# mLSTM by chunks of 128 tokens with a carried state, in a hybrid decoder layer on one core

## The chip, the core and the metric

The kernel runs on one NeuronCore of a Trainium2 chip (trn2). Time is device microseconds (us) of one execution. The engines are TensorE (matmuls into the eight PSUM banks), VectorE, ScalarE and GpSimd (element work) and SyncE (SP), which here only issues DMAs. Each runs its own instruction queue in order; they meet at semaphores. The input is one sequence of 512 tokens of width 1024, all of it float32.

## What is computed

One decoder layer. The normalised input is projected once (`z = rms_norm(x) @ w_in`, 2964 columns) and split between three mixers: MoBA attention (4 heads of 64), an mLSTM (4 heads, q and k of 64, v of 128) and NSA attention (4 query heads of 64; compressed, selected and window branches). Their outputs are normalised by head, projected by `w_out`, and a squared-ReLU MLP of width 4096 follows. The change concerns the mLSTM. By head, with `logf` the log sigmoid of the forget gate and `ig` the input gate:

```
bcum = cumsum(logf)
D[t,s] = bcum[t] - bcum[s] + ig[s]              for s <= t
m[t]  = max(running maximum carried in, max_s D[t,s])
S[t,s] = (q_t . k_s / 8) * exp(D[t,s] - m[t])
hid_t = sum_s S[t,s] v_s / max(|sum_s S[t,s]|, exp(-m[t]))
y_ml  = head_norm(hid) * g * sigmoid(lo)
```

The reference states the same thing in chunks of 64: within a chunk the products above, and for everything earlier a state `C = sum_s exp(...) v_s k_s^T` (128 x 64, and its row for the denominator) that is decayed and added to from chunk to chunk, and multiplied with q_t and a weight of t.

## The kernel before

Tokens lie in NT = 4 tiles of 128. Every engine has one function (`@block.tensor`, `@block.vector`, `@block.scalar`, `@block.gpsimd`, `@block.sync`) in which all its work stands in the order in which it runs; nothing plans it, and the position of a call in these functions is its place in the engine's queue. A wait (`wait_ge`) holds all that is behind it on that engine.

Large float32 products are made of three products of rounded halves (fp32r), `mm3` (lines 1748 to 1752): each weight chunk is loaded into `raw` by SP, ScalarE writes its high half (`high_half`, line 763) and GpSimd the difference (`low_half`, line 661). The mixers' q and k get halves in the same way: `nq_high`/`nq_low` and `moba_high`/`moba_low`, and SP copies halves from one half of the partitions to the other (lines 559 to 604). SP's order is: chunk c of `CHUNK_ORDER`, where chunk c waits for the low half of chunk c - 2 (line 516), the four copies to `nq_st` ahead of `C_WO + 2`, then the MoBA copies in the order of `MB_ORDER` (k, k, q, q, k, k, q, q), then the MLP's weights. TensorE's first MoBA score waits for the first four of these and their low halves (`score`, line 1913).

The input projections are "jobs", each in PSUM bank job % 8; `bank_free(n)` makes TensorE wait until the reader of job n - 8 (`READER`) has read. Around the change TensorE does: MQ (two jobs of 24 matmuls), `spread` 0 and 1 (the running maximum m of a head, put on all partitions), MK, `spread` 2 and 3, the 64 products of the compression MLP, and then mLSTM in eight units u = (pair of heads p, token tile i):

- `ml_scores(u)` (line 1888): for each j <= i and both heads the 128 x 128 tile k_j . q_i;
- VectorE multiplies with the decay tiles `exp(gcol[s] - m[t])` into `probsT` (line 1409). ScalarE made these for all j <= i (line 873), GpSimd masks the diagonal ones (line 696);
- `ml_values(u)` (line 1899): for each j <= i and both heads `probsT_j` times v_j with a column of ones (129 columns), summed in PSUM;
- ScalarE copies to `hid` (`ml_evict`) and sums squares (`ml_squares`).

Between these units stand the rest of the compression (`fold`, GELU, the two small products with `w2k` and `w2v` in unit 3), the compressed attention scores (after unit 4), and the first four scores of attention. On ScalarE the high halves of w_out chunks 0 and 1 (`C_WO`, `C_WO + 1`) stand in units 3 and 4, and on GpSimd their low halves come right after `nq_low`.

Then comes the attention loop over 24 units (six pairs of heads, four token tiles each): scores, row maximum on VectorE, exponential on ScalarE, transposes, copies of them (one on VectorE, one on ScalarE, `copy_t`), and per pair values, a transposition back and the output. Pairs 0 to 3 are NSA's, pairs 4 and 5 MoBA's. In its first units the loop also carries the compressed branch (`cmp_transposes`, `cmp_out`, `cmp_gated`) and the mLSTM's divisors (`ml_divisors`, unit 2) and reciprocal roots (units 3 and 4). Their last product is the scale factors by which GpSimd multiplies `hid` and `y` (lines 726 to 732), and in ScalarE's queue `moba_high` of the q halves waits for these. After the loop come w_out's projection and the MLP.

## Time and profile before

| | us |
|---|---|
| median of 3 runs (612.62 to 613.42) | 612.93 |
| the profiled execution | 612.87 |
| its span, first to last instruction | 611.1 |
| TensorE busy, 3158 matmuls | 598.2 (98%) |
| VectorE busy | 384.7 (63%) |
| ScalarE busy | 303.1 (50%) |
| GpSimd busy | 258.3 (42%) |

Busy time of TensorE counts the pipelined end of each matmul, so it is not TensorE at its peak. An fp32 matmul has two records in the trace, an fp32r or bf16 matmul and a transpose one. In a timeline, neighbouring instructions of one kind are merged (x16), and the length of a merged line reaches to the end of its last instruction, which overlaps the start of the next line.

### The profile page before, as it was taken

The numbers are of one execution on the slowest core, as the hardware profiler recorded it, in microseconds if no ns is written. First come the engines' busy times: TensorE is split into PE (matmuls) and PEld (weight loads), VectorE is DVE, ScalarE is ACT, GpSimd is POOL, SyncE is SP. The second block draws the span as 40 slices with busy tenths as digits, with TensorE's granted clock in tenths as the row PEclk, the third lists the DMA queues.
The fourth block names the chain that finished last, engine by engine and source line by source line (L and its number), as shares of the span: only waits on it lengthen the run. The fifth ranks groups of instructions, "written<-read, shape, count | busy, mean of one in ns | idle before, by whom it ended". The sixth has DMA issues, their size and how long they took to land.

```text
span 611.1 us, 8442 instructions
## 1 busy us (share of the span) xinstructions
PE 598.2 (98%) x3158; PEld 491.5 (80%) x3158; DVE 384.7 (63%) x650; ACT 303.1 (50%) x551; POOL 258.3 (42%) x149
## 2 busy tenths in 40 slices
PE   8999999999999999999999999999999999999995
PEld 5898888877866678889888888888888888888884
DVE  6414505216787883883899868577495685771657
ACT  7613424237868952564564625545445255453322
POOL 8553413614837430053159372533722725711611
PEclk9999999999999999999999999999999999999998
DMA  9743272345412230025225070440612503204002
GB/s 331 279 151 121 96 180 86 69 104 173 146 28 65 74 105 1 0 70 201 77 86 190 24 252 0 146 130 1 213 62 110 166 2 137 70 1 168 4 35 104
DMA packets 36004, 65.08 MB, mean 106 GB/s; under 512 B 2812, under 2 KB 23548, under 8 KB 34940
## 3 DMA queue, kind: packets, MB, share of 16 engines
q1 hardware_dynamic: 35660, 64.15, 32.7%
q8 instruction: 25, 0.41, 0.3%
q10 hardware_dynamic: 304, 0.39, 0.2%
q14 instruction: 15, 0.12, 0.1%
HBM read 60.08 MB, written 2.10 MB: 102 GB/s over the span
## 4 chain that ended last, share of the span: by engine, by line
PE 91%; DVE 4%; issue 2%; ACT 1%; DMA 1%; SPq 0%; POOLq 0%; POOL 0%; DVEq 0%; ACTq 0%
PE ps L1750 20%; PE ps L1752 20%; PE ps L1751 20%; PE ps L2156 7%; PE ps L2158 7%; PE ps L2157 7%; PE ps L2028 2%; PE ps L2013 1%; PE ps L1908 1%; ACT probs L942 1%; DMA x_land<-in_x_turned 1%; PE ps L1932 1%; PE ps L1933 1%; DVE probsT L1409 1%; PE ps L1884 1%
## 5 line engine op out<-in xcount | busy, mean ns | idle before, releaser
L1750 PE MATMUL ps<-xT_h,ring_h 128*128 128x512 f32 (+1 forms) x384 | 143.6, 374 | 0.0
L1752 PE MATMUL ps<-xT_h,ring_l 128*128 128x512 f32 (+1 forms) x384 | 143.2, 373 | 0.0
L1751 PE MATMUL ps<-xT_l,ring_h 128*128 128x512 f32 (+1 forms) x384 | 143.1, 373 | 0.0
L747 POOL TENSOR_TENSOR ring_l<-raw_d,ring_h 128x1024 fp32r<-128x1024 f32 x25 | 67.3, 2699 | 129.8 <-ACT ring_h L1021 129.8
L747 POOL TENSOR_TENSOR ring_l<-raw,ring_h 128x1024 fp32r<-128x1024 f32 x31 | 76.7, 2501 | 77.6 <-DVE xres L1566 38.1
L667 POOL TENSOR_TENSOR ring_l<-raw,ring_h 128x512 fp32r<-128x512 f32 (+2 forms) x26 | 64.1, 2486 | 77.3 <-ACT ring_h L772 77.3
L1660 DVE TENSOR_TENSOR y<-ps,y 128x512 f32<-128x512 f32 x90 | 61.1, 688 | 51.0 <-PE ps L2158 50.7
L1750 PEld LDWEIGHTS ps<-xT_h,ring_h 128*128 128x128 f32 x384 | 72.4, 188 | 13.1 <-issue 0.4
L1752 PEld LDWEIGHTS ps<-xT_h,ring_l 128*128 128x128 f32 x384 | 72.4, 188 | 12.9
L1751 PEld LDWEIGHTS ps<-xT_l,ring_h 128*128 128x128 f32 x384 | 72.4, 189 | 12.8
L2156 PE MATMUL ps<-ring_h,a_h 128*128 128x512 f32 x196 | 76.7, 391 | 0.1
L2158 PE MATMUL ps<-ring_h,a_l 128*128 128x512 f32 x196 | 76.4, 390 | 0.0
L2157 PE MATMUL ps<-ring_l,a_h 128*128 128x512 f32 x196 | 76.4, 390 | 0.0
L1750 PE MATMUL ps<-ring_h,xT_h 128*128 128x512 f32 (+1 forms) x158 | 61.0, 386 | 0.3 <-DVE xT_l L1222 0.3
L1752 PE MATMUL ps<-ring_h,xT_l 128*128 128x512 f32 (+1 forms) x158 | 60.3, 381 | 0.0
L1751 PE MATMUL ps<-ring_l,xT_h 128*128 128x512 f32 (+1 forms) x158 | 60.2, 381 | 0.0
L1021 ACT ACTIVATE ring_h<-raw 128x1024 fp32r<-128x1024 f32 x32 | 33.1, 1057 | 22.8 <-PE ps L2158 19.1
L2156 PEld LDWEIGHTS ps<-ring_h,a_h 128*128 128x128 f32 x196 | 36.8, 188 | 8.5 <-issue 0.8
L1058 ACT ACTIVATE ps<-ps 128x512 f32<-128x512 f32 x32 | 18.7, 583 | 50.1 <-PE ps L1752 50.1
L2158 PEld LDWEIGHTS ps<-ring_h,a_l 128*128 128x128 f32 x196 | 36.8, 188 | 8.0
L2157 PEld LDWEIGHTS ps<-ring_l,a_h 128*128 128x128 f32 x196 | 36.8, 188 | 7.7
L772 ACT ACTIVATE ring_h<-raw 128x2048 fp32r<-128x2048 f32 (+1 forms) x14 | 26.0, 1858 | 27.0 <-PE ps L1752 16.2
(264 smaller groups left out, 1012.3 us busy)
## 6 DMA issues: line engine op xcount, KB each, us to landing
raw<-in_w_mlp SPq DMA_DIRECT2D x16, 1024.0 KB, 5.5
raw_d<-in_w_mlp SPq DMA_DIRECT2D x16, 1024.0 KB, 6.0
raw<-in_w_groups SPq DMA_DIRECT2D x8, 1024.0 KB, 4.8
raw<-in_nsa_cmp_w SPq DMA_DIRECT2D x8, 512.0 KB, 6.6
raw<-in_w_groups SPq DMA_DIRECT2D x8, 256.0 KB, 5.2
xres<-in_x SPq DMA_DIRECT2D x4, 512.0 KB, 7.2
raw<-in_w_out SPq DMA_DIRECT2D x2, 1024.0 KB, 7.3
raw<-in_w_out SPq DMA_DIRECT2D x4, 512.0 KB, 4.6
```

The costliest lines, as they stand in the source:

```text
L667: last = nc.gpsimd.tensor_tensor(ring_l[r][:, a:a + step], raw[c % RAW][:, a:a + step], ring_h[r][:, a:a + step].bitcast(F32), ALU.subtract)
L747: nc.gpsimd.tensor_tensor(slot(ring_l, n), slot_source(n), slot(ring_h, n).bitcast(F32), ALU.subtract).then_inc(lo_done, 1)
L772: nc.scalar.activation(ring_h[r][:, 0:n], raw[c % RAW][:, 0:n], ACT.Copy).then_inc(hi_done, 1)
L1021: nc.scalar.activation(slot(ring_h, n), slot_source(n), ACT.Copy).then_inc(hi_done, 1)
L1058: nc.scalar.activation(tile, tile, ACT.Relu).then_inc(relu_ready, 1)
L1660: nc.vector.tensor_tensor(ya, ps[:, product_bank(b, k) + s, :], ya, ALU.add).then_inc(acc_ready, 1)
L1750: nc.tensor.matmul(o, sh, mh, start=start, stop=False)
L1751: nc.tensor.matmul(o, sh, ml, start=False, stop=False)
L1752: return nc.tensor.matmul(o, sl, mh, start=False, stop=stop)
L2156: nc.tensor.matmul(o, ah, wh[:, q, :], start=fresh and q == 0, stop=not fresh, **go_on)
L2157: nc.tensor.matmul(o, ah, wl[:, q, :], start=False, stop=not fresh, **go_on)
L2158: last = nc.tensor.matmul(o, al, wh[:, q, :], start=False, stop=not fresh or q == 1, **go_on)
```

## The change

The mLSTM's pairs of different token tiles (j < i) are replaced by a state. For each head and each of the first three chunks (NCH = 3) the change forms the chunk's sum of k times v with weights relative to m at the chunk's end (`mend`), adds it to the decayed state before it, and multiplies the state with q times `exp(mend - m[t])` (`q_far`). The diagonal tiles (j = i) stay as they are, now with one decay tile per head and tile (`W`).

- Projection part: the order on TensorE is MQ's first half, all four `spread`, MQ's second half, six transposes of k (`key_transposes`), the diagonal score tiles (`near_scores`), MK's first half, the states (`states`), MK's second half, compression. The job numbers and thereby the PSUM banks and their readers are new.
- ScalarE makes four decay tiles and three exponentials in place in PSUM for each head; VectorE the differences of m at chunk ends, `q_far`, the weighted keys `k_tok`, the product of near scores and decay in place in `W`, and the carried states.
- mLSTM part: `ml_values(u)` is one near product and (i > 0) one far product a head. Two units share one eviction; ScalarE copies to `hid` and writes squares to `hid_sq`, and VectorE sums them (`ml_sums`).
- Compression: GELU, the products with `w2k` and `w2v` and the compressed values come after all mLSTM units and after the first four attention scores. The compressed scores are in one bank (bank 6), with full-height products, inside the attention loop behind the first transposes; their maxima and probabilities on VectorE are in units 0 and 1 of the loop, `cmp_transposes` and `cmp_out` behind steps 4, 6 and 8 instead of 1, 3 and 6, `cmp_gated` in units 3 and 4 instead of 2 and 3.
- w_out's chunks: ScalarE's high half of chunk 0 is behind the second eviction, that of chunk 1 in loop unit 4. GpSimd's low halves of chunks 0 and 1 stand behind the mLSTM's normalisation. The first two `moba_high` are in loop units 1 and 3.

The diff, cut to what the prediction speaks of:

```diff
+J_LV, J_B, J_CONV, J_LO, J_LI, J_LF, J_KV, J_KS, J_NQ, J_GC, J_SP, J_KT, J_SC, J_ST, J_H = (
+    0, 4, 8, 12, 16, 17, 18, 19, 20, 22, 24, 29, 31, 36, 39)
+J_MQ, J_MK = (23, 28), (35, 38)
+HT_BANK = 7
...
-READER = "vvvv" "vvvv" "vvvv" "aaaa" "v" "v" "v" "v" "vv" "a" "vv" "aa" "vv" "aa" "vv"
+READER = "vvvv" "vvvv" "vvvv" "aaaa" "v" "v" "v" "v" "vv" "a" "v" "vvvv" "v" "vv" "vvvv" "v" "vv" "v" "vv"
...
-ML_BANK = [2, 0]
+ML_BANK = [3, 5, 3, 5]
...
-CT_S, CO_S = 1, (3, 6)
+CS_S, CT_S, CO_S = 0, 4, (6, 8)
...
-                last.then_inc(w_ready, 1)
-            pool.wait_ge(w_ready, HEADS)
-            nq_low(2)
-            nq_low(3)
-            low_half(C_WO)
-            low_half(C_WO + 1)
+                nc.gpsimd.affine_select(out=W[:, h], in_=W[:, h], compare_op=ALU.is_ge, fill=0.0, base=0,
+                                        pattern=[[0, NT], [1, P]], channel_multiplier=-1).then_inc(w_ready, 1)
+            for h in range(HEADS):
+                nq_low(h)
+
...
-            pool.wait_ge(lo_done, split_no(C_WO) + 2)
             for n in range(2):
                 moba_low(n)
 
@@ -730,6 +736,9 @@
                 pool.wait_ge(ml_h, t + 1)
                 yml = y[:, t, 256:768].rearrange("p (h d) -> p h d", h=HEADS)
                 nc.gpsimd.tensor_tensor(yml, yml, hid[:, t, :, 0:DV], ALU.mult).then_inc(ml_y, 1)
+            low_half(C_WO)
+            low_half(C_WO + 1)
+            pool.wait_ge(lo_done, split_no(C_WO) + 2)
             for n in range(2, 2 * HEADS):
...
-                act.wait_ge(job_done, J_MB[h] + 1)
-                for j in range(NT):
-                    last = nc.scalar.activation(decay(h, slice(j, NT), j),
-                                                ps[:, J_MB[h] % 8, j * P:SEQ].rearrange("p (i t) -> p i t", t=P),
-                                                ACT.Exp, scale=-1.0, bias=gcol[:, j, h:h + 1])
-                last.then_inc(read_a, 1)
-                act.wait_ge(read_a, reads(J_MB[h])[1])
-                nc.scalar.activation(zero1[:], zero1[:], ACT.Copy).then_inc(w_exp, 1)
...
+                r, held = half_rows(h % 2), ps[:, (J_SP + h) % 8, :]
+                act.wait_ge(job_done, J_SP + h + 1)
+                act.wait_ge(mend_ready, h + 1)
+                for i in range(NT):
+                    last = nc.scalar.activation(W[:, h, i, :], held[:, i * P:(i + 1) * P], ACT.Exp, scale=-1.0,
+                                                bias=gcol[:, i, h:h + 1])
+                last.then_inc(w_exp, 1)
+                act.wait_ge(w_exp, h + 1)
+                for i in range(1, NT):
+                    last = nc.scalar.activation(held[r, i * P:(i + 1) * P], held[r, i * P:(i + 1) * P], ACT.Exp, scale=-1.0,
+                                                bias=mend[r, h, i - 1:i])
+                last.then_inc(far_ready, 1)
+            nc.scalar.activation(factor[:], factor[:], ACT.Exp).then_inc(factor_ready, 1)
+            act.wait_ge(job_done, J_MK[1] + 1)
...
+            for h in range(HEADS):
+                nq_high(h)
+            act.wait_ge(dup_in, 32)
+            for k, keys_ in enumerate((kselT, kwinT)):
+                nc.scalar.activation(nk_st[:, k, :], keys_[:], ACT.Copy).then_inc(nk_hi, 1)
+
...
+            def ml_evict(v):
+                p, i = ml_place(v)
+                act.wait_ge(ml_o, v + 1)
+                nc.scalar.activation(hid[:, i:i + 2, 2 * p:2 * p + 2, :], ml_pair(v, DV + 1), ACT.Copy)
+                if v >= 2:
+                    act.wait_ge(ml_ss, v - 1)
+                nc.scalar.activation(hid_sq[:, v % 2], ml_pair(v, DV), ACT.Square).then_inc(ml_used, 1)
...
-            for u in range(len(ML_UNITS)):
-                if u >= 1:
-                    ml_evict(u - 1)
-                if u == 1:
+            for v in range(4):
+                if v == 3:
                     act.wait_ge(gelu_arg, 1)
                     nc.scalar.activation(cg[:, 3], cg[:, 2], ACT.Exp, scale=-1.5957691216057308).then_inc(gelu_exp, 1)
-                if u == 3:
-                    act.wait_ge(kv_cmp, 1)
-                    nc.scalar.activation(kcT[:], ps[:, 4, 0:NP_], ACT.Copy).then_inc(kc_ready, 1)
-                if u in (3, 4):
-                    high_half(C_WO + u - 3)
-                if u == 5:
-                    act.wait_ge(cs_sub, 1)
-                    nc.scalar.activation(cexp[:], cexp[:], ACT.Exp).then_inc(cs_exp, 1)
-                if u >= 1:
-                    ml_squares(u - 1)
-                if u >= 6:
-                    moba_high(u - 6)
+                ml_evict(v)
+                if v == 1:
+                    high_half(C_WO)
...
             exp(0)
-            ml_evict(len(ML_UNITS) - 1)
+            act.wait_ge(kv_cmp, 2)
+            for m in range(2):
+                last = nc.scalar.activation(kc2[half_rows(m), m, :], ps[half_rows(m), 6, 0:NP_], ACT.Copy)
+            last.then_inc(kc_ready, 1)
             exp(1)
...
                 if u == 0:
+                    act.wait_ge(cs_sub, 1)
+                    nc.scalar.activation(cexp[:], cexp[:], ACT.Exp).then_inc(cs_exp, 1)
+                if u in (1, 3):
+                    moba_high(u // 2)
+                if u == 4:
+                    high_half(C_WO + 1)
+                if u == 2:
...
+            for h in range(HEADS):
+                p, m = divmod(h, 2)
+                r, bank = half_rows(m), (J_SP + h) % 8
+                dve.wait_ge(job_done, J_SP + h + 1)
+                link(nc.vector.tensor_copy(mend[:, h, :], ps[:, bank, P - 1:NCH * P:P]))
+                nc.vector.tensor_tensor(into[:, :, h], gcol[:, 0:NCH, h], ps[:, bank, P - 1:NCH * P:P], ALU.subtract)
+                nc.vector.tensor_tensor(on[r, p, :], ps[r, bank, P - 1:2 * P:P], mend[r, h, 1:NCH], ALU.subtract
+                                        ).then_inc(mend_ready, 1)
+            for h in range(HEADS):
+                p, r = h // 2, half_rows(h % 2)
+                dve.wait_ge(far_ready, h + 1)
+                nc.vector.tensor_tensor(q_far[p][r, :], ps[r, (J_SP + h) % 8, P:SEQ], qkT[r, p, P:SEQ], ALU.mult).then_inc(read_v, 1)
...
+            for h in range(HEADS):
+                dve.wait_ge(job_done, J_SC + h + 1)
+                dve.wait_ge(w_ready, h + 1)
+                nc.vector.tensor_tensor(W[:, h], ps[:, (J_SC + h) % 8, :].rearrange("p (i t) -> p i t", t=P), W[:, h],
+                                        ALU.mult).then_inc(read_v, 1)
...
-            for u, (p, i) in enumerate(ML_UNITS):
-                w = (i + 1) * P
-                for m in range(2):
-                    s, h = 2 * u + m, 2 * p + m
-                    dve.wait_ge(ml_s, u + 1)
-                    dve.wait_ge(w_ready, h + 1)
-                    if s >= 3:
-                        dve.wait_ge(ml_o, (s - 3) // 2 + 1)
-                    nc.vector.tensor_tensor(probsT[:, s % 3, 0:w].rearrange("p (j t) -> p j t", t=P),
-                                            ps[:, ML_BANK[u % 2] + m, 0:w].rearrange("p (j t) -> p j t", t=P),
-                                            decay(h, i, slice(0, i + 1)), ALU.mult).then_inc(ml_p, 1)
...
+            def ml_sums(v):
+                p, i = ml_place(v)
+                c = SS_ML + HEADS * i
+                dve.wait_ge(ml_used, v + 1)
+                nc.vector.tensor_reduce(stat[:, c:c + 2 * HEADS].rearrange("p (i h) -> p i h", h=HEADS)[:, :, 2 * p:2 * p + 2],
+                                        hid_sq[:, v % 2], AX.X, ALU.add).then_inc(ml_ss, 1)
+
+            ml_sums(0)
+            gelu()
+            ml_sums(1)
+            gelu_rest()
+            ml_sums(2)
+            ml_sums(3)
             row_max(0)
             row_max(1)
-            cmp_probs()
+            cmp_values()
             row_max(2)
...
-                if u in (2, 3):
-                    cmp_gated(u - 2)
+                if u == 0:
+                    cmp_max()
+                if u == 1:
+                    cmp_probs()
+                if u in (3, 4):
+                    cmp_gated(u - 3)
...
             def spread(h):
 
-                bank_free(J_MB[h])
-                if h == 0:
-                    pe.wait_ge(m_ready, 2)
...
+                bank_free(J_SP + h)
+                nc.tensor.matmul(ps[:, (J_SP + h) % 8, :], sel[:, h, :], m_split[:, 0, :], start=True, stop=False)
+                nc.tensor.matmul(ps[:, (J_SP + h) % 8, :], sel[:, h, :], m_split[:, 1, :], start=False, stop=True).then_inc(job_done, 1)
...
+                for i in range(NT):
+                    t = slice(i * P, (i + 1) * P)
+                    for m in range(2):
+                        r = half_rows(m)
+                        last = nc.tensor.matmul(ps[:, (J_SC + 2 * p + m) % 8, t], qkT[r, 2 + p, t], qkT[r, p, t], start=True, stop=True)
+                        if i == NT - 1:
+                            last.then_inc(job_done, 1)
...
+                for c in range(NCH):
+                    for m in range(2):
+                        h = 2 * p + m
+                        last = nc.tensor.matmul(ps[half_rows(m), (J_ST + p) % 8, (DV + 1) * c:(DV + 1) * (c + 1)],
+                                                k_tok[:, c, DH * h:DH * h + DH], lv1[:, c, h, :], start=True, stop=True)
+                last.then_inc(job_done, 1)
+
+            half_feature(J_MQ[0], C_MQ, 0)
+            pe.wait_ge(m_ready, 2)
+            for h in range(HEADS):
+                spread(h)
+            half_feature(J_MQ[1], C_MQ, 1)
+            pe.wait_ge(silu_done, 4)
+            key_transposes(0)
+            key_transposes(1)
+            near_scores(0)
+            near_scores(1)
+            half_feature(J_MK[0], C_MK, 0)
+            states(0)
+            states(1)
+            half_feature(J_MK[1], C_MK, 1)
+
...
-                pe.wait_ge(ml_p, 2 * u + 2)
-                if u == 1:
-                    pe.wait_ge(*reads(J_MB[3]))
-                if u >= 2:
-                    pe.wait_ge(ml_used, u - 1)
+                t = slice(i * P, (i + 1) * P)
+                if u in (4, 6):
+                    pe.wait_ge(ml_used, u // 2 - 1)
...
                 for m in range(2):
-                    for j in range(i + 1):
-                        last = nc.tensor.matmul(ps[:, 7 - u % 2, 256 * m:256 * m + DV + 1],
-                                                probsT[:, (2 * u + m) % 3, j * P:(j + 1) * P],
-                                                lv1[:, j, 2 * p + m, :], start=(j == 0), stop=(j == i))
-                last.then_inc(ml_o, 1)
+                    h = 2 * p + m
+                    last = nc.tensor.matmul(ml_tile(u, DV + 1)[:, m, :], W[:, h, i, :], lv1[:, i, h, :], start=True, stop=i == 0, **far)
...
+                        last = nc.tensor.matmul(ml_tile(u, DV + 1)[:, m, :], q_far[p][r, (i - 1) * P:i * P], state[r, p, i - 1, :],
+                                                start=False, stop=True, skip_group_check=True)
+                if u % 2:
+                    last.then_inc(ml_o, 1)
...
-            pe.wait_ge(read_v, reads(J_H)[1])
+            pe.wait_ge(*reads(J_MK[1]))
+            for u in range(4):
+                ml_values(u)
+            pe.wait_ge(*reads(J_H))
...
-
-            for u in range(len(ML_UNITS)):
-                if u + 1 < len(ML_UNITS):
-                    ml_scores(u + 1)
-                if u == 3:
...
+            for u in range(4, len(ML_UNITS)):
                 ml_values(u)
-                if u == 4:
-                    pe.wait_ge(kc_ready, 1)
...
-                if u == 6:
-                    pe.wait_ge(nk_lo_ready, 2)
-                    pe.wait_ge(nq_in, 16 * HEADS)
-                    pe.wait_ge(ml_p, 14)
-                    score(0)
-                    score(1)
-                if u == 7:
-                    score(2)
-                    score(3)
+            pe.wait_ge(nk_lo_ready, 2)
+            pe.wait_ge(nq_in, 16 * HEADS)
+            for s in range(4):
+                if s == 1:
+                    pe.wait_ge(ml_used, 3)
+                score(s)
+            pe.wait_ge(ml_used, 4)
+            pe.wait_ge(gelu_ready, 1)
...
+            def cmp_scores():
+                pe.wait_ge(kc_ready, 1)
+                pe.wait_ge(vc_ready, 1)
+                nc.tensor.matmul(ps[:, 6, :], identb[:], mask_c[:, :, 0:1, :].to_broadcast([P, NT, HEADS, NP_]), start=True, stop=True)
+                for i in range(NT):
+                    for p in range(2):
+                        c = (HEADS * i + 2 * p) * NP_
+                        last = nc.tensor.matmul(ps[:, 6, c:c + 2 * NP_], nqT[:, p, i * P:(i + 1) * P],
+                                                kc2[:].rearrange("p m n -> p (m n)"), start=False, stop=True, skip_group_check=True)
+                last.then_inc(cs_done, 1)
 
...
+                    if s == CS_S:
+                        cmp_scores()
                     if s == CT_S:
                         cmp_transposes()
                     if s in CO_S:
```

## Rows read from the trace of the kernel before

**Rows 1.** The page's busy time of each engine.
```profile
PE 598.2 (98%) x3158; PEld 491.5 (80%) x3158; DVE 384.7 (63%) x650; ACT 303.1 (50%) x551; POOL 258.3 (42%) x149
```

**Rows 2.** The page's chain of waits that ended last, by engine.
```profile
PE 91%; DVE 4%; issue 2%; ACT 1%; DMA 1%; SPq 0%; POOLq 0%; POOL 0%; DVEq 0%; ACTq 0%
```

**Rows 3.** Busy us by stage: PE, PEld, DVE, ACT, POOL, then PEclk, DMA share, GB/s.
```profile
142.00:164.00 22.00, 20.98 (x213) 18.74 (x214) 15.92 (x41) 15.33 (x49) 14.64 (x15) 1.00 0.45 138
...
176.60:197.50 20.90, 18.52 (x139) 12.83 (x136) 17.35 (x39) 16.72 (x49) 16.88 (x14) 1.00 0.19 45
197.50:221.80 24.30, 23.68 (x181) 16.91 (x180) 19.30 (x44) 22.15 (x60) 10.00 (x8) 1.00 0.38 109
```

**Rows 4.** Groups of TensorE instructions: line, shapes, count, busy us, mean ns.
```profile
L1908 PE MATMUL ps<-lv,probsT 128*128 128x129 f32 x80 | 11.1, 285 | 1.0 <-DVE probsT L1409 0.8
...
L1895 PE MATMUL ps<-qkT 64*128 64x128 f32 x80 | 6.6, 292 | 0.0
...
L1976 PE MATMUL ps<-kcT,nqT 64*128 64x32 f32 x32 | 2.0, 274 | 0.0
```

**Rows 5.** Timeline of TensorE, 137 to 165 us: start, length, line, records.
```profile
137.28 3.68 PE L1884 MATMUL ps<-raw,blk 64*32 64x256 f32 x128
140.90 0.49 PE L1895 MATMUL ps<-qkT 64*128 64x128 f32 x4
...
151.26 2.05 PE L1908 MATMUL ps<-lv,probsT 128*128 128x129 f32 x16
...
158.50 1.16 PE L1895 MATMUL ps<-qkT 64*128 64x128 f32 x16
...
164.61 0.42 PE L1932 MATMUL ps<-nk_st,nq_st 128*128 128x384 f32 x1
```

**Rows 6.** Timeline of ScalarE, 126 and 151 us.
```profile
126.69 1.76 ACT L873 ACTIVATE W_own<-ps,gcol 128x512 f32<-128x512 f32 x4
...
150.83 1.90 ACT L772 ACTIVATE ring_h<-raw 128x2048 fp32r<-128x2048 f32 x1
```

**Rows 7.** Timeline of VectorE, 148 to 177 us.
```profile
147.95 0.22 DVE L1337 TENSOR_SCALAR cg<-cg 128x128 f32<-128x128 f32 x1
...
149.65 0.36 DVE L1343 COPY gelr<-gel 128x128 f32<-128x128 f32 x2
...
177.00 0.17 DVE L1513 TENSOR_TENSOR stat<-stat,den 128x16 f32<-128x16 f32 x1
```

**Rows 8.** Timeline of GpSimd, 152 to 190 us.
```profile
152.87 9.89 POOL L667 TENSOR_TENSOR ring_l<-raw,ring_h 128x512 fp32r<-128x512 f32 x8 [6.51 <-ACT ring_h L772]
...
177.32 1.04 POOL L729 TENSOR_TENSOR hid<-hid,stat 128x512 f32<-128x512 f32 x1 [11.31 <-DVE stat L1513]
...
185.67 1.19 POOL L732 TENSOR_TENSOR y<-y,hid 128x512 f32<-128x512 f32 x1
186.82 2.67 POOL L718 TENSOR_TENSOR mq_lo<-mqT,mq_st 64x512 fp32r<-64x512 f32 x2
```

**Rows 9.** Timeline of TensorE, the first MoBA score.
```profile
197.52 0.36 PE L1932 MATMUL ps<-mk_st,mq_st 128*128 128x256 f32 x1
```

**Rows 10.** Timeline of SP's DMA issues, 166 to 190 us.
```profile
166.54 0.60 SPq L598 DMA_DIRECT2D mk_odd<-mk_odd  x1
188.13 1.85 SPq L602 DMA_DIRECT2D mq_st<-mq_lo  x2
```

**Rows 11.** DMA issues: target, source, count, KB, median us to landing.
```profile
mk_odd<-mk_odd SPq DMA_DIRECT2D x1, 128.0 KB, 4.4
...
nq_st<-nq_lo SPq DMA_DIRECT2D x4, 128.0 KB, 5.5
...
mq_st<-mq_lo SPq DMA_DIRECT2D x4, 128.0 KB, 2.2
```

**Rows 12.** The same columns at the end; the third last is PEclk.
```profile
604.00:605.00 1.00, 0.62 (x6) 0.42 (x4) 0.97 (x3) 0.73 (x1) 0.72 (x1) 1.00 0.91 340
...
606.00:607.00 1.00, 0.00 (x0) 0.00 (x0) 0.81 (x4) 0.16 (x1) 0.00 (x0) 0.80 0.00 0
```

257 lines of the change are left out of this document (110 added, 147 removed).

## The prediction, as it was written before the result

> **What bounds the kernel now.** I read the page's busy shares first. TensorE is busy for 598.2 of 611.1 us [rows 1] and the chain that ended last lies on it for 91% [rows 2], so time is won only where TensorE gets shorter or where its few waits go. The profiled execution took 612.87 us, 1.8 us more than its span; the median of the three runs is 612.93, so the sum can be made against 612.87. Second came the busy time by stage. The mLSTM stretch (142 to 164 us) has TensorE busy for 20.98 of 22.00 us; the first pairs of attention (176.6 to 197.5) for 18.52 of 20.90; the last ones, to the output projection, for 23.68 of 24.30 [rows 3]. The reader is to see that nothing idles for long, and that the attention loop has VectorE, ScalarE and GpSimd at 65% to 90% as well: work that is put into the loop finds little room. Third I read the order of each queue by the timelines, because this kernel has every order written out by hand, and the change moves work past other work on GpSimd.
>
> **TensorE's own work.** Removed: 40 score products and 40 value products, each an fp32 matmul in two records, 80 + 80 records. A run of 16 value records takes 2.05 us, of which the last one's 0.28 overlaps: about 0.12 us a record, 9.6 us in all; 16 score records take 1.16 us because two 64-row products run side by side: 0.06 us a record, 4.8 us in all [rows 4, 5]. Added: 16 near scores (32 records, 1.9 us), 16 near values (32 at 0.12, 3.8 us), 12 far values in 64-row pairs (24 at 0.06, 1.4 us), 12 state products, 64 columns wide, side by side as the scores are (24 at 0.06, 1.4 us; 2.8 if they don't overlap), 6 transposes (0.11 each, 0.7 us). That is 14.4 against 9.2: 5.2 us less. The compressed scores go from 32 records in 2.0 us [rows 4] to 16 full-height records that I put at 0.12 each, equal. With these numbers alone the kernel would end near 607.7.
>
> **The projection part.** Transposes, near scores and states now stand before the compression: +4.3 us with a switch of operand type, so compression ends at about 145.3 instead of 141.0 [rows 5]. New waits there: the MK bank of the first half is the bank of the last spread, and is free only when VectorE has multiplied the last head's exponentials with q. ScalarE does seven exponentials of 128 columns a head; four with 1280 columns together took 1.76 us [rows 6], so at most 2.0 us a head, from 120.1 (spread done) to 128.1, VectorE until 128.7; TensorE comes to it at 128.9. Hidden, with 0.2 us to spare; without that cover up to 2 us are lost. VectorE's mends, key and decay products (some 6 us) lie beside 11 us of the two MK halves, on an engine with long waits there; nothing for that. The masks on GpSimd are one 512-column instruction instead of four small ones: nothing.
>
> **From compression to the loop.** TensorE has 2.75 (units 0 to 3) + 1.0 (fold) + 2.75 (units 4 to 7) + 1.45 (scores 0 to 3) = 8.0 us to do: it would be at 153.3. What is late is the GELU chain, which lay beside mLSTM work before. The exponential of GELU stands on ScalarE behind three double evictions (about 1.2 us each, copy and square) and behind the 1.90 us high half of the first w_out chunk [rows 6]: I get 153.3 for its end. VectorE's rest of GELU lasts from 147.95 to 150.0 in the trace, 2.05 us [rows 7]: 155.4. Then the two small products (1.2), VectorE's last two sums of squares, row maxima and four copies of compressed values (3.5 us with the wait for the first softmax exponential): 158.9, where TensorE can begin the compressed scores (2.2). From here VectorE is the chain: maxima and subtraction 1.3, unit 1 of attention 1.6, compressed probabilities 2.0, units 2, 3 and 4 with divisors, gated sums and reciprocal roots 2.4 + 3.4 + 3.2. That puts the mLSTM scale factors (stat, line 1513) at 175.0; before they are there at 177.2 [rows 7]. So of 5.2 us some 2 are left by then; the others are turned into waits of 1 to 2 us each. Bounds: 169.3 if none of these waits is there (154.5 for the loop's start, 12.6 from there to the factors as between 164.61 and 177.2 [rows 5, 7], 2.2 for the compressed scores); 177.5 if the loop keeps the length it has. The wait for nq_st: the last copy is issued at about 147.8 and takes 2.2 us (as on an empty queue) to 5.5 [rows 11], TensorE asks at 151.9; up to 1.4 us, inside these bounds.
>
> **GpSimd's order: the term that decides.** Before, the low halves of the first two w_out chunks ran on GpSimd at 152.87 to 162.8, 9.89 us beside the mLSTM [rows 8]. Now they stand behind the mLSTM normalisation and ahead of the low halves of MoBA's queries. Normalisation starts when the factors are there and takes from 177.32 to 186.86, 9.5 us; then, before, the two q halves follow at once and TensorE reads the first MoBA score at 197.52 [rows 8, 9], 5.4 us after their copies landed (two issued from 188.13 to 189.98, 2.2 us each [rows 10, 11]). After: 175.0 + 0.1 + 9.5 = 184.6; two low halves, 10.0: 194.6. This holds SP too. Its queue has w_out chunk 3 behind the low half of chunk 1, and all MoBA copies behind that. Before, chunk 3 was issued at 162.8, and the last of the four MoBA copies behind it went out at 166.54 and landed 4.4 us later, at 170.9: 8.1 us after the release [rows 10, 11]. After, six copies are behind it instead of four, but they don't wait for GpSimd in between: 8 to 9 us, I take 8.3. The last q copy lands at 194.6 + 8.3 = 202.9. TensorE would come to that score at about 196: it stands for 6 to 7 us, and the score is at 202.9 instead of 197.52, +5.4. Behind it the order is as before: 24.3 us to the projection with TensorE 97% busy, so next to nothing is caught up; w_out chunks 2 and 3 keep 4 us of slack, as ScalarE and GpSimd shift with the loop.
>
> **The clock.** In the trace the granted clock is at 2.4 GHz (1.00) through all working stretches; after the last matmul, over at 604.6, it falls to 1.2 GHz within 606 to 607: that slice has 0.80 [rows 12]. The new stop is three times as long as those 2 us, so I expect the fall inside it. What it costs afterwards no row shows; from nothing (it rises at once) to 3 us (half speed for as long as the stop lasted). I take 0.8.
> The Trainium skill (TensorE: Matmul & The Clock Gate, What's actually happening) says that the throttled state is the default and activity releases it, so work resumes slow. By that rule the cost is above nothing, and the sum moves toward the upper half of my range; the trace agrees as to the fall.
>
> Sum: 612.87 + 5.4 + 0.8 = **619.1 us**.
>
> **The rivals.**
> *The saving reaches the end.* The 5.2 us, perhaps less 1 or 2 for new waits: 607.7 to 611.5, faster. For it speaks TensorE's 98%. It needs the last q copy by 197.5 - 3, thus the factors by 167, while even without a wait they come at 169.3. It decides only if GpSimd's 9.5 + 10.0 us or the 8.3 behind them shrink by 5 us. 8%.
> *Neither way.* Factors at 169.3 to 170 and a quick landing give 612 to 613.5. 4%.
> *The stop is there but short.* Factors at 171 to 173, copies 7.5 us after the release, no fall of the clock: +1.5 to +3.5, 614 to 616.4. 18%.
> *The stop and more.* The exponentials on ScalarE take longer than 2.0 us a head, TensorE stands before MK and the whole chain shifts; or the clock costs its 3 us: 621.5 to 624. 10%.
> *As summed*, 60%, with its own range of 616.5 to 621.5.
>
> **How the numbers follow.** The likeliest is 619.1. A range of 614.5 to 622.3 holds the sum's own range, most of the short stop and a part of the long one, and leaves out the two cases below it and the top. What a measurement of this kernel tells from no change is about 0.2%, 1.2 us (611.7 to 614.1). Faster is the first rival, 8%; the same 4%; slower 88%.
>
> **What would show it.** Right: TensorE idle by 5 us or more before the first score with mk_st, ended by a transfer (mq_st); GpSimd's two low halves between the normalisation and mq_lo; SP's w_out chunk 3 issued at about 194.6; the granted clock under 1.00 just there; factors at 173 to 177; compression over at 145 to 146; a wait before the products that read gel, and one before the compressed scores. Wrong: MoBA's first score before 198, a wait over 1 us in the projections, or mLSTM records that cost more than 0.12 us.

## The result: slower, 623.03 us

The changed kernel takes 623.03 us (622.18 to 626.64, four runs) against 612.77 for the kernel before on the same chip: ratio 1.0177, 95% interval 1.0136 to 1.0218. The forecast was 619.1 with a range to 622.3, so the direction and the place of the loss were forecast, and the time lies 0.7 us above the range. The profiled execution took 622.87 us, 10.0 more than that of before.

The busy shares of the page come first, as in [rows 1]:
```profile
PE 596.7 (96%) x3099; PEld 489.2 (79%) x3099; DVE 388.9 (63%) x665; ACT 299.8 (48%) x529; POOL 257.1 (41%) x137
```
TensorE is busy for only 1.5 us less, to which the lower clock described below adds some 3.6, and its share falls from 98% to 96%. The chain of waits has new members beside it; in [rows 2] GpSimd had no share:
```profile
PE 87%; POOL 4%; DMA 3%; DVE 2%; issue 2%; ACT 1%; SPq 1%; POOLq 0%; ACTq 0%; DVEq 0%
```
Where it is lost, the timelines of GpSimd and of SP's queue show, from the mLSTM normalisation on (compare [rows 8, 10]):
```profile
175.75 1.04 POOL L735 TENSOR_TENSOR hid<-hid,stat 128x512 f32<-128x512 f32 x1 [1.69 <-DVE stat L1546]
...
184.12 1.18 POOL L738 TENSOR_TENSOR y<-y,hid 128x512 f32<-128x512 f32 x1
185.26 10.40 POOL L683 TENSOR_TENSOR ring_l<-raw,ring_h 128x512 fp32r<-128x512 f32 x8
195.73 2.61 POOL L725 TENSOR_TENSOR mq_lo<-mqT,mq_st 64x512 fp32r<-64x512 f32 x2
```
```profile
190.28 6.28 SPq L543 DMA_DIRECT2D raw<-in_w_out  x4
196.61 1.11 SPq L609 DMA_DIRECT2D mk_st<-mk_st  x2
...
199.06 1.24 SPq L618 DMA_DIRECT2D mq_st<-mq_lo  x2
```
and TensorE's at the first MoBA score (197.52 without a wait in [rows 9]):
```profile
205.50 0.55 PE L2000 MATMUL ps<-mk_st,mq_st 128*128 128x256 f32 x1 [9.30 <-DMA mq_st<-mq_lo]
```
The low halves of w_out stand between the normalisation and the MoBA queries, w_out's loads between them and the copies, and TensorE idles for 9.30 us. The score is 8.0 us late. Then comes the clock. The columns are as in [rows 3], the third last is the granted clock:
```profile
196.00:205.50 9.50, 0.20 (x3) 0.03 (x1) 1.69 (x3) 1.74 (x6) 7.30 (x6) 0.70 0.93 243
205.50:208.00 2.50, 2.50 (x13) 2.31 (x13) 1.14 (x3) 0.78 (x2) 0.00 (x0) 0.50 0.50 125
208.00:209.50 1.50, 1.50 (x10) 1.41 (x9) 0.42 (x1) 0.84 (x3) 0.00 (x0) 0.50 0.00 0
209.50:211.00 1.50, 1.50 (x13) 1.45 (x12) 0.63 (x2) 0.46 (x2) 0.00 (x0) 0.83 0.00 0
```
TensorE resumes at 1.2 GHz and stays there for about 4.5 us. A transposition of y, first in the kernel before and then here, starts 9.8 us late, so 1.8 us came after the score:
```profile
227.88 1.03 PE L2043 MATMUL ps<-ident,y 128*128 128x128 f32 x8
```
```profile
237.71 1.03 PE L2099 MATMUL ps<-ident,y 128*128 128x128 f32 x8
```
8.0 + 1.8 are the 10.0 but for 0.2.

The same columns for the projections show a second fall, which I did not foresee. The last line is the kernel before, which has 1.00 in each of the three stretches:
```profile
118.00:121.00 3.00, 3.00 (x13) 1.95 (x12) 2.20 (x13) 1.18 (x5) 3.00 (x2) 1.00 0.10 17
121.00:124.00 3.00, 3.00 (x9) 2.32 (x9) 0.93 (x3) 2.94 (x12) 1.26 (x3) 0.55 0.42 125
124.00:127.00 3.00, 3.00 (x14) 2.39 (x13) 0.85 (x2) 2.93 (x12) 0.78 (x2) 0.89 1.13 223
```
```profile
121.00:124.00 3.00, 3.00 (x15) 2.22 (x13) 0.00 (x0) 0.00 (x0) 0.08 (x1) 1.00 0.47 115
```
TensorE is busy throughout. What is new just before is that all eight matmuls of `spread`, which have four rows, stand in a row (the first at 118.43), where before they stand in two groups of four. Eight of the matmuls after them are 0.43 us apart instead of 0.23, and the compression ends at 146.9 instead of the predicted 145.3.

### The profile page after: what moved, and what is told of

The parts are those of the page before. It is cut to its first block, busy times and chain, and to the rows that moved or that the text cites. A ratio compares the mean times of both kernels' runs of the same rounds, so it can differ in the third digit from the quotient of the medians.

```text
span 621.1 us, 8286 instructions
## 1 busy us (share of the span) xinstructions
PE 596.7 (96%) x3099; PEld 489.2 (79%) x3099; DVE 388.9 (63%) x665; ACT 299.8 (48%) x529; POOL 257.1 (41%) x137
## 4 chain that ended last, share of the span: by engine, by line
PE 87%; POOL 4%; DMA 3%; DVE 2%; issue 2%; ACT 1%; SPq 1%; POOLq 0%; ACTq 0%; DVEq 0%
PE ps L1783 20%; PE ps L1785 20%; PE ps L1784 20%; PE ps L2212 7%; PE ps L2214 7%; PE ps L2213 7%; POOL ring_l L683 2%; PE ps L2069 1%; DMA nq_st<-nq_lo 1%; DMA mq_st<-mq_lo 1%; POOL nq_lo L700 1%; POOL y L738 1%; PE ps L2084 1%; POOL hid L735 1%; DMA x_land<-in_x_turned 1%
## 5 line engine op out<-in xcount | busy, mean ns | idle before, releaser
L1020 ACT ACTIVATE ring_h<-raw 128x1024 fp32r<-128x1024 f32 x32 | 33.1, 1056 | 22.8 <-PE ps L2214 19.3
```

The costliest lines, as they stand in the source:

```text
L1020: nc.scalar.activation(slot(ring_h, n), slot_source(n), ACT.Copy).then_inc(hi_done, 1)
```

## The experiments

Theory A is the prediction's: the place of the two low halves on GpSimd, and of w_out's loads on SP, makes the stop. Rival B: one of the two orders alone decides. Theory F came with the trace: matmuls of four rows and new waits let the clock fall. Theories C, D, E, G and others are named in the expectations. "Before" in each result is the kernel before on the same chip, and a ratio is against it. Each kernel has one profile, of one of its executions.

**The one move by itself, in the kernel before.** The low halves go behind the normalisation; nothing else of the change is in it.
```diff
             nq_low(3)
-            low_half(C_WO)
-            low_half(C_WO + 1)
...
-            pool.wait_ge(lo_done, split_no(C_WO) + 2)
             for n in range(2):
                 moba_low(n)
...
+            low_half(C_WO)
+            low_half(C_WO + 1)
+            pool.wait_ge(lo_done, split_no(C_WO) + 2)
             for n in range(2, 2 * HEADS):
                 moba_low(n)
```


> The kernel before, with the low halves of w_out chunks 0 and 1 moved on GpSimd behind the mLSTM normalisation, and nothing else. Theory A (this one move makes the stop, whatever form the mLSTM has): factors at 177.2, normalised at 186.8, low halves until 197.2, last q copy 9.8 us later at 207: first MoBA score at 206.5 to 207.5 instead of 197.5, then 1.2 GHz for some 4.5 us: 623 to 625.5 us. Rival D (the stop needs the new mLSTM order too): 613 to 617 us.

Measured: 624.27 us against 612.87, ratio 1.018 (1.0165 to 1.0195). TensorE's timeline in it:
```profile
206.69 0.55 PE L1932 MATMUL ps<-mk_st,mq_st 128*128 128x256 f32 x1 [9.14 <-DMA mq_st<-mq_lo]
```
Two calls in another place, with the wait that belongs to them, make the whole loss (11.4 us here, 10.3 for the change), stop and slow clock (0.50 from 204 to 212) with it; what else the change does adds nothing to it on balance.

**GpSimd's order alone.** In the changed kernel `moba_low(2)` and `moba_low(3)` go ahead of the low halves.

> The changed kernel, with the low halves of MoBA's first two q heads moved ahead of the two w_out low halves on GpSimd; SP's order is left. Theory A (two gates: GpSimd's order, and SP's queue in which the copies stand behind w_out chunk 3): the q halves are ready at 188 but the copies still wait for the low half of w_out chunk 1, which is 2.7 us later (198.4): first MoBA score at 206 to 208.5, 623 to 626 us. Rival B (GpSimd's order alone): the stop is gone, score at 196, 611 to 613 us.

Measured: 626.44, ratio 1.0206 (1.0172 to 1.0240). The query halves are done at 187.7, and the score is later still, at 208.29 after a stop of 12.28 us: SP's copies stand behind w_out chunk 3, whose release is now 2.5 us later.

**SP's order alone.** The first four heads' copies go ahead of the loads of w_out chunks 2 and 3.

> The changed kernel, with the first four heads' MoBA copies moved ahead of w_out chunks 2 and 3 in SP's queue; GpSimd's order is left. Theory A: the copies wait only for the q low halves (198.3), score at 200.5 to 202.5, a stop of 4 to 6 us instead of 9.3: 617 to 620 us. Rival B: SP's order is no gate, 622 to 623.5 us as before. Rival C (the transfers themselves are slow whatever stands before them, 4 to 6 us): score at 203 to 204, 620 to 621.5.

Measured: 621.49 (619.40 to 622.80), ratio 1.0123 (1.0091 to 1.0156), above the 617 to 620 of theory A. The stop is halved all the same:
```profile
204.53 0.55 PE L2005 MATMUL ps<-mk_st,mq_st 128*128 128x256 f32 x1 [4.55 <-DMA mq_st<-mq_lo]
```
With no load and no other copy ahead of them the two q copies land 2.2 us after their issue, so the transfers are not slow by themselves, as rival C had it. The time gains less than the stop, because the profiled execution has a slow clock at 157 to 168 besides (0.50 in 162 to 168), and reaches the score's place 3.8 us later than the changed kernel's does.

**Both orders.**

> Both moves together. Theory A: the first MoBA score comes at 196 without a stop or a fall of the clock; the second pair's k and q (low halves now at 198.4 to 203.6, copies behind w_out chunk 3) are late by 2 to 4 us for the fifth pair's first score at about 205: 612.5 to 616.5 us. Rival (the stop has another cause, such as the mLSTM factors or the loop's own pace): 619 us or more.

Measured: 618.24 (612.63 to 621.37, ten runs), ratio 1.0062 (1.0030 to 1.0095), above the 612.5 to 616.5 expected. The score comes at 198.69 with no wait. Rival B falls: there are two gates. With GpSimd's order alone the stop grows to 12.28 us, with SP's alone it is 4.55, with both it is gone. A smaller one has moved to the second MoBA pair, as expected:
```profile
210.37 0.35 PE L2007 MATMUL ps<-mk_st,mq_st 128*128 128x256 f32 x1 [2.43 <-DMA mq_st<-mq_lo]
```
The runs spread over 9 us, and they go by the clock: the mean granted clock was 0.997 and 0.998 in those of 613.29 and 612.63, 0.981 in that of 621.37. In the profiled one (618.6) the clock is 0.50 from 157 to 168, a third place, and again at 212 to 214, behind that wait.

**The low halves early, as in the kernel before.** In the changed kernel they come right behind `nq_low`, with the second high half behind the fourth eviction on ScalarE.
```diff
             for h in range(HEADS):
                 nq_low(h)
+            low_half(C_WO)
+            low_half(C_WO + 1)
...
                 if v == 1:
                     high_half(C_WO)
+                if v == 3:
+                    high_half(C_WO + 1)
...
-                if u == 4:
-                    high_half(C_WO + 1)
...
-            low_half(C_WO)
-            low_half(C_WO + 1)
```


> The changed kernel, with both w_out low halves back where they were, ahead of MoBA's first low halves on GpSimd, and ScalarE's high half of chunk 1 behind the fourth mLSTM eviction (ScalarE is idle there for 2.0 us). Theory A: no stop at the first MoBA score, which comes at 196 to 197 (197.52 before the change): 610.5 to 612.5 us, the mLSTM work's own gain less its new waits. Rival D (the mLSTM change itself costs time, and the loop is slowed by it): over 613.5 us. Rival E (low halves beside VectorE's GELU chain slow that chain by 1 to 2 us, as both work out of SBUF): 612.5 to 614.

Measured: 614.77 (613.99 to 616.57), ratio 1.0022 (1.0008 to 1.0036); score at 198.41, no stop. The loss against the kernel before shrinks from 10.3 us to 1.4 by this alone. It is not the gain that theory A expected (610.5 to 612.5). What rival E feared shows in the profile: the two copies that write gelr take 2.31 us instead of 0.36. The third fall is there as well, and these rows show what TensorE did before it (columns as above):
```profile
153.00:157.00 4.00, 1.95 (x16) 1.48 (x16) 3.83 (x7) 2.89 (x3) 4.00 (x5) 0.97 0.04 14
157.00:162.00 5.00, 4.42 (x19) 3.78 (x19) 3.88 (x13) 2.32 (x10) 4.82 (x4) 0.50 0.63 210
162.00:168.00 6.00, 6.00 (x30) 4.86 (x30) 3.22 (x6) 2.21 (x7) 0.00 (x0) 0.58 0.57 175
```
It stood for half of 153 to 157, waiting for nq_st (1.14 us) and for the GELU values (1.05). The waits alone don't settle it: the changed kernel has 1.14 and 0.94 us there, and 1.00 behind them.

**The clock in the stop.** In the changed kernel, 36 matmuls of 128 rows by 512 columns that nobody reads stand in front of the wait.

> The changed kernel, with 36 matmuls of 512 columns (8 us at 2.4 GHz) put on TensorE in front of its wait for the first MoBA score; their result is overwritten. Theory (after the stop TensorE works at 1.2 GHz from 205.5 to about 210, and that costs 2.2 us beside the wait itself): the first MoBA score still comes at 205 to 206, the granted clock stays 1.00 there, 620 to 621.5 us. Rival (what follows the stop is bound by the copies behind it, so the clock costs nothing): 622.5 to 623.5 us.

Measured: 620.68, ratio 1.0114 (1.0085 to 1.0143). The clock is 1.00 from 196 on. The two executions with a mean clock of 0.998 took 619.11 and 619.14; I take it that the clock fell nowhere in them. In the other two (622.21, 623.33) it was 0.99, and the profiled one, the last, has the fall at 157 to 168 and so comes late to the stop:
```profile
208.09 0.36 PE L2003 MATMUL ps<-mk_st,mq_st 128*128 128x256 f32 x1 [0.78 <-DMA mq_st<-mq_lo]
```
From this score to the end of the span it takes 413.5 us, as before the change (413.6), and the changed kernel takes 415.6: the slow clock behind the stop costs 2.0 us. Without any slow clock the changed kernel is 6.2 us slower than before, and the slow clock makes some 3.8 of its 10.

The third fall can be priced in the same way. From the first attention score to the mLSTM factors the changed kernel takes 19.2 us and the one with GpSimd's order alone 19.3, both without that fall; this one (156.16 to 178.35) takes 22.2, those with SP's order and with both orders 21.9 and 22.8: about 3 us.

**Four rows against 128 rows, in the kernel before.** 16 more matmuls are put into its spreads, in one kernel copies of the spread's own (4 rows), in the other products of x with 128 rows, both 512 columns:
```diff
+                for _ in range(2):
+                    nc.tensor.matmul(ps[:, J_MB[h] % 8, :], sel[:, h, :], m_split[:, 0, :], ...)
+                    nc.tensor.matmul(ps[:, J_MB[h] % 8, :], sel[:, h, :], m_split[:, 1, :], ...)
```
```diff
+                for _ in range(4):
+                    nc.tensor.matmul(ps[:, J_MB[h] % 8, :], xT_h[:, 0, 0:P], xT_h[:, 0, :], ...)
```


> The kernel before, with four more matmuls of 4 rows and 512 columns in each spread (16 in all, twelve such matmuls in a row at 124 and at 137 us); their result is overwritten. TensorE's own time grows by 16 x 0.227 = 3.6 us. Theory F (a run of 4-row matmuls lets the granted clock fall, as at 121.3 us of the changed kernel, and each fall costs 1.6 us): granted clock under 1.00 behind one or both runs, 618 to 620 us. Rival (the number of rows is nothing to the clock): 616.0 to 616.9 us, clock 1.00.

> The same as the kernel before with sixteen more matmuls in the spreads, but of 128 rows. Theory F and its rival: 616.0 to 616.9 us with the clock at 1.00 throughout. If the clock falls here as well, it is the place or the number of matmuls and not their rows.

Measured: 618.08 (615.95 to 619.01) with four rows and 616.52 (616.46 to 616.99) with 128; before 612.87. 16 matmuls at a step of 0.23 are 3.7 us, which is all that the second one costs. The four executions of the first have mean clocks of 0.992 to 0.997, and the one of 0.997 (615.95) is no slower than the second kernel's, so the fall isn't in each of them. The windows of the first show the rest, in a stretch in which TensorE is always busy:
```profile
124.00:127.00 3.00, 3.00 (x13) 2.12 (x12) 0.69 (x1) 1.22 (x3) 0.00 (x0) 0.94 1.14 226
127.00:131.00 4.00, 4.00 (x12) 3.02 (x12) 0.00 (x0) 2.64 (x8) 2.13 (x8) 0.62 0.51 141
```
and those of the second:
```profile
124.00:127.00 3.00, 3.00 (x12) 1.75 (x11) 0.69 (x1) 1.23 (x3) 0.00 (x0) 1.00 1.13 221
127.00:131.00 4.00, 4.00 (x18) 3.02 (x18) 0.00 (x0) 2.64 (x8) 2.14 (x8) 1.00 0.53 151
```

**The spreads taken apart.** As with the low halves early, and spreads 2 and 3 each stand between groups of MQ's second half.
```diff
                                xT_h[:, k, :], xT_l[:, k, :], k == 0, k == NC - 1)
+                    if k in between:
+                        spread(between[k])
...
-            for h in range(HEADS):
+            for h in range(2):
                 spread(h)
-            half_feature(J_MQ[1], C_MQ, 1)
+            half_feature(J_MQ[1], C_MQ, 1, {1: 2, 3: 3})
```


> The changed kernel with the two low halves of w_out early on GpSimd (as in e4_early_low, 614.8 us), and the last two of the four spreads taken apart: each stands between two groups of the second half of MQ instead of all eight four-row matmuls in a row. Theory F (a row of four-row matmuls lets the granted clock fall): clock 1.00 from 118 to 131 in the profile, compression over at 145.3 or before; but the fall at 157 to 168 stays, and the time with it: 613.5 to 615. Rival (the place of the spreads says nothing of the clock): a clock of 0.5 to 0.6 at 121 to 124 is as likely as in the changed kernel.

Measured: 614.45, ratio 1.0032 (1.0019 to 1.0044). The clock is 1.00 from 118 to 157 and 0.50 at 160 to 168, as expected. One profile doesn't show that the first fall is gone for good: the kernel with the low halves early had none there in its own, either. All profiles together say more. With the eight matmuls in a row four of seven have it (0.50 to 0.61 in 121 to 124: the changed kernel, GpSimd's order alone, SP's alone, and the first filled kernel below), with the spreads taken apart none of six.

**The waits filled.** Small bf16 products that nobody reads stand in three of TensorE's waits, without and with the spreads taken apart.
```diff
+            def fill(n, bank, c0=0):
+                for _ in range(n):
+                    nc.tensor.matmul(ps[:, bank, c0:c0 + 256], identb[:], mask_c[:].rearrange("p i a n -> p (i a n)"), start=True, stop=True)
+
+            fill(9, 2)
             pe.wait_ge(nk_lo_ready, 2)
...
+            fill(9, 6)
             pe.wait_ge(gelu_ready, 1)
...
+                fill(7, 6)
                 pe.wait_ge(cs_ready, 1)
```


> e4_early_low with TensorE kept at work in three of its waits by products that nobody reads (bf16, 128 rows by 256 columns: nine ahead of score(0), nine ahead of the products that read gel, seven ahead of the transposes of the compressed probabilities, about 0.11 us each, so about as long as the waits they stand in: 1.14, 1.05 and 1.05 us). Theory C: the clock falls at 157 to 168 because TensorE had stood twice just before; with the waits filled it stays at 1.00, TensorE gets back 2 to 4 us there, first MoBA score at 195 to 197, time 610.5 to 613. Rival D: VectorE is the chain there and a slow TensorE costs next to nothing: 614 to 616, first MoBA score at 198. Rival E: the clock falls in spite of the filling; 614 to 616 with 0.50 in some of the windows of 154 to 170.

> Both of the above together. Theory: clock 1.00 throughout, 610 to 612.5, faster than before (612.8 to 613.4), because the 5.2 us less of TensorE's work then reach the end less the waits of the compressed branch. Rival D or E: 614 to 616 as without filling.

Measured: 613.28 (ratio 1.0005, 0.9993 to 1.0017) and 612.92 (1.0001, 0.9991 to 1.0011). The clock stays at 1.00 from 154 to 170 in both profiles, where it fell in those of the two kernels without fillers (it was still 0.992 or less as a mean in four and two of the eleven executions). So theory C is borne out for this place, but the filling gives back 0.9 and 1.5 us against the kernel before, not 2 to 4, and both times lie above the expected ones (610.5 to 613, 610 to 612.5): with the clock held the kernel is only as fast as before, and the mLSTM factors come at 177.3, no sooner than in [rows 7]. (The first of the two has the fall at 121 to 124 in its profile, 0.61.) Where a part of the saving stays, VectorE's timeline of the second kernel shows:
```profile
155.54 0.29 DVE L1385 TENSOR_TENSOR gel<-cg 128x128 f32<-128x128 f32 x1
155.91 0.06 DVE L1387 MEMSET gel<- 128x4 f32 x1
156.00 2.29 DVE L1389 COPY gelr<-gel 128x128 f32<-128x128 f32 x2
```
Two copies that took 0.36 us in [rows 7] take 2.29, beside GpSimd's low halves. My repair had brought a collision of its own.

**Products instead of copies**, with two fillers instead of nine ahead of the GELU values; and **the query copies ahead of w_out's second load** on SP besides.
```diff
-                    last = nc.vector.tensor_copy(gelr[:, t], gv[:, t, 1:2, :].to_broadcast([P, HEADS, NP_]))
+                    src = gv[:, t, 1:2, :].to_broadcast([P, HEADS, NP_])
+                    last = nc.vector.tensor_tensor(gelr[:, t], src, src, ALU.max)
...
-                if c == C_WO + 2:
+                if c == C_WO + 1:
                     for h in range(HEADS):
                         p, m = divmod(h, 2)
```


> e12_early_apart_filled with the two copies of the GELU values (VectorE, line 1389) written as products of the two operands' maximum (tensor_tensor of the values with themselves, same result), and two fillers instead of nine ahead of the products that read gel. Theory P (the two copies take 2.3 us instead of 0.36 because GpSimd works on the low halves of w_out beside them, and tensor_tensor doesn't suffer from it): 0.6 us for the two in the profile, values of GELU ready at 156.7 instead of 158.3, mLSTM factors at 175.6 instead of 177.3, time 611 to 612. Rival (only the copies get quicker, the wait for nq_st before score(0) is late instead): factors at 177, 612.5 to 613.5.

> e13_products, and on SP the four copies of the low halves of the attention's queries ahead of the load of the second w_out chunk instead of behind it; fillers 2, 5 and 7. Theory W (these copies take 7.6 us instead of 2.2 to 5.5 because 1 MB of w_out is ahead of them in the same queues): landing 3 to 5 us, score(0) at 154.5 without a wait over 0.3 us, factors at 174 to 175.5, first MoBA score at 194.5 to 196, time 609.5 to 611.5, faster than before by 0.2 to 0.5%. Rival (the factors hang on the GELU chain alone, score(0) may come at 157 at no cost): as e13_products within 0.5 us.

Measured: 613.98 (1.0018, 1.0004 to 1.0031) and 614.99 (1.0035, 1.0021 to 1.0049). Both theories failed; they had expected 611 to 612 and 609.5 to 611.5. The two instructions last 2.4 us as well:
```profile
155.86 2.41 DVE L1390 TENSOR_TENSOR gelr<-gel 128x128 f32<-128x128 f32 x2
```
In the second kernel the nq_st copies land in 3.9 us instead of 7.1, and nothing comes of it, as TensorE then waits for the GELU values. With fewer fillers ahead of these the clock fell in both (0.50 at 162 to 166).

**GpSimd out of the way.** The low halves wait until the GELU values are written; VectorE copies as in the changed kernel, spreads apart, waits filled (9, 5 and 7 products). And the same with the query copies first (2, 5 and 7 products).
```diff
             for h in range(HEADS):
                 nq_low(h)
+            pool.wait_ge(gelu_ready, 1)
             low_half(C_WO)
```


> e12_early_apart_filled with GpSimd starting the two low halves of w_out only when VectorE has written the GELU values (one more wait on GpSimd), and five fillers instead of nine ahead of the products that read gel. ScalarE's high half of the second chunk stays where it was. Theory G (GpSimd beside them is what makes the two small VectorE instructions that write gelr last 1.2 us each instead of 0.22): 0.36 us for the two, GELU values ready at 156.4, low halves 156.5 to 166.5, mLSTM factors at 175.5, 610.5 to 611.8. Rival H (it is ScalarE's high half, at 155.7 to 157.6 beside them, or something else): still 2.3 us for the two, factors at 177, 612.5 to 613.5.

> e15_low_after_gelu, and on SP the four copies of the low halves of the attention's queries ahead of the load of the second w_out chunk, fillers 2, 5 and 7. If the wait for nq_st is still on the path once the GELU values come early: 0.3 to 1 us under e15_low_after_gelu. If the GELU chain is the only bound: equal within 0.4 us, or slower where the clock falls because fewer fillers stand before it.

Measured: 612.06 (610.82 to 613.09, eleven runs) against 613.13, ratio 0.9980 (0.9972 to 0.9989), and 611.73, ratio 0.9982 (0.9971 to 0.9994): faster than before by 0.2%, both, and not to be told apart. The first one's VectorE and GpSimd, and below them ScalarE's high half:
```profile
155.51 0.36 DVE L1390 COPY gelr<-gel 128x128 f32<-128x128 f32 x2
```
```profile
156.01 9.92 POOL L683 TENSOR_TENSOR ring_l<-raw,ring_h 128x512 fp32r<-128x512 f32 x8 [7.18 <-DVE gelr L1390]
```
```profile
155.22 1.92 ACT L780 ACTIVATE ring_h<-raw 128x2048 fp32r<-128x2048 f32 x1
```
ScalarE is still beside the copies and GpSimd no longer is, and they take 0.36 us: it was GpSimd (theory G). The factors are done at 175.6, and the first MoBA score is at 195.91 instead of 197.52; the time is 0.3 us above the 610.5 to 611.8 expected.

The Trainium skill (SBUF — State Buffer, Who interferes with whom) has this collision: VectorE's copies in a two-port mode, and its instructions with both inputs in SBUF, take a port pair that GpSimd needs too, and whoever comes second is blocked for a whole instruction. The 1.2 us for each agree, and it says why the products did not help. The product at 155.54, with two inputs in SBUF beside the same GpSimd work, took its usual 0.29, which this rule doesn't explain.

## Why the prediction was right and wrong

- **GpSimd's order decides: right**, and the order of the calls is the cause (the one move alone gives 624.27). The factors are written at 175.4 (175.0 forecast), the low halves last until 195.66 (194.6), then come SP's loads and the copies, and a stop ended by mq_st with a slow clock.
```profile
175.43 0.17 DVE L1546 TENSOR_TENSOR stat<-stat,den 128x16 f32<-128x16 f32 x1
```

- **From the release to the last q copy: the step that failed, a term that was too small.** 8.3 us were taken, 9.8 measured (195.66 to 205.50). I had taken the 8.1 of before and 0.2 for two more copies. The last q copy goes out 4.0 us after the release (3.7 before), but lands 5.7 us later, not the 4.4 of [rows 11]: it has five others of its size and 1 MB of w_out ahead of it. Where nothing was ahead, with SP's order changed, such a copy took 2.2 us; how much of the rest is the loads' and how much the copies' no run tells. With 0.4 us from the factors, 0.2 from the start of the normalisation behind them (the 9.5 for itself were right) and 0.4 from the low halves (10.4 instead of 10.0) the score is at 205.5 instead of 202.9: 2.6 of the 3.8 us missed.
- **The clock: the second step that failed, in size and in place.** "What it costs afterwards no row shows ... I take 0.8": it cost 1.8 to 2.0 after the stop, 1.0 us more than taken. And that TensorE's clock can fall while it is busy I did not consider; the fall at the spreads put the compression 1.6 us late. Without any fall the time is 619.1, the number predicted, but that is luck. By my estimate the factors would then come at about 173.8 (175.4 less the 1.6) instead of 175.0; these 1.2 us and the 0.8 for the clock, which would not be spent, cancel the 2.1 that the copies' landing, the low halves and the start of the normalisation add. This is the most that the factors can gain: in the profiles of both orders and of the filled stop, which lack the first fall, TensorE waits longer for nq_st (1.88 and 2.26 us instead of 1.14) and makes its first attention score only 0.8 and 0.05 us sooner.
- **"Hidden, with 0.2 us to spare"** held: q_far was done at 128.25, TensorE came to MK at 130.4 and would have come 1.6 us sooner without the fall, still after it. In the kernel with the low halves early, whose profile has no fall there, compression ends at 145.1 (145.3 predicted).
- **TensorE's own work: right to about 1 us, with errors on both sides.** The timeline of TensorE in the changed kernel:
```profile
148.33 0.71 PE L1972 MATMUL ps<-lv,W 128*128 128x129 f32 x4
148.97 0.49 PE L1976 MATMUL ps<-state,q_far 64*128 64x129 f32 x4
149.40 0.71 PE L1972 MATMUL ps<-lv,W 128*128 128x129 f32 x4
```
  From start to start four near records take 0.64 us, 0.16 each instead of 0.12, and four far ones, 64 rows and put at 0.06, take 0.43, 0.11 each. The eight units take 7.3 us instead of 5.5. It is the price of short runs, and they were dear before too: there 4, 8, 12 and 16 value records take 0.65, 1.09, 1.53 and 1.98 us, and 4 and 16 score records 0.45 and 1.09. So what was removed was priced too low as well, from its longest runs. In the kernel before:
```profile
143.74 0.71 PE L1908 MATMUL ps<-lv,probsT 128*128 128x129 f32 x4
144.39 0.94 PE L1895 MATMUL ps<-qkT 64*128 64x128 f32 x12
```
  The last kernel, whose clock is 1.00 in every stretch of 112 to 225 us, gives the balance:
```profile
PE 595.8 (98%) x3113; PEld 487.5 (80%) x3113; DVE 388.6 (64%) x665; ACT 299.4 (49%) x529; POOL 257.0 (42%) x137
```
  Its 14 fillers are about 1.5 us of that, so TensorE's own work is 3.9 us less than the 598.2 of before. Of these the fillers take 1.5 and longer waits 0.9, and the profiled span is 1.5 us shorter. That is why the best version gains 0.2% and not more; in the result the stop hid it.
- **From compression to the loop: right.** There is a wait at the first score (1.14 us) and one before the compressed scores (0.94), and the factors are within 0.5 us. This too is in part luck: the compressed scores start 1.4 us later than I had, and the loop from there to the factors takes 15.2 us instead of 16.1. The wait before gel isn't in the profile of the changed kernel; with the low halves early it was there (1.05). And one reading of [rows 3] was wrong: in its last stretch GpSimd is at 41%, not at 65% or more. No term of the sum used it.

What stays open: why the clock falls in some executions of a kernel and not in others, and at which of the three places. The runs give a price for each place (1.6 us at the compression's end, 2.0 behind the stop, about 3 at 157 to 168) and, by the spreads and the fillers, something that goes along with it; the cause is not shown.

## What to carry to other kernels

A call that moves in a hand-written order must be followed through every queue that waits for it: here 10 us of element work, which had idle time of GpSimd to hide in (16.83 us in one piece ahead of MoBA's first keys in the changed kernel), was put onto the one stretch where two engines' queues and a transfer stood behind it. When a change makes TensorE's work sparse (few rows, short waits), look at the granted clock of each stretch in several executions before anything else: 9 us of spread in one kernel went with it. And a repair is a change like any other: the early low halves ran into VectorE's copies until one more wait on GpSimd kept them apart.

## What was not expected of the hardware

The granted clock fell to 1.2 GHz with TensorE busy without a gap, after eight four-row matmuls in a row (0.55 in 121 to 124 us) and again after twelve (0.62 in 127 to 131); sixteen more matmuls with 128 rows in the same places left it at 1.00. The fall is in some executions only. The Trainium skill (TensorE: Matmul & The Clock Gate, HAM oscillation — how this bites in real kernels) tells of falls by idle gaps, which agrees with the 9.3 us stop; for falls without a gap the runs here stand by themselves.

Two VectorE instructions of 128 columns lasted 1.05 to 1.35 us each beside GpSimd's tensor_tensor, as copies and as products; the copies last 0.22 without it.
